# Five steps of a hybrid RWKV-7 and GLA trunk layer, moved between VectorE, ScalarE and GpSimd

## The chip, the cores and the metric

The program runs on one core of one Trainium2 chip. The metric is the device time of one execution in microseconds. Three runs of the kernel before took 932.28, 933.67 and 936.69 us; their median is 933.67.

## What is computed

One layer is computed for 128 context tokens and 512 latent tokens (640 in all, width 1024). In it the input projection is split into channels for an RWKV-7 mixer and a GLA mixer:

```python
def rwkv_mixer(r, k, v, lw, la, lg, s0, grid, p):
    rkv = short_conv(jnp.concatenate([r, k, v], axis=-1), p['rw_conv'], grid)   # 3x3 over the grid, or 3 taps
    r, k, v = jnp.split(rkv, 3, axis=-1)
    kk = heads(k * p['rw_k_k'])
    kk = kk * lax.rsqrt(jnp.sum(kk * kk, axis=-1, keepdims=True) + EPS)
    for d in range(2):
        w = jnp.exp(-RW_DECAY_SCALE * jax.nn.sigmoid(p['rw_w0'][d] + jnp.tanh(lw[d]) @ p['rw_w2'][d]))
        a = jax.nn.sigmoid(p['rw_a0'][d] + la[d] @ p['rw_a2'][d])
        ...
    bonus = (jnp.sum(rh * kh * p['rw_r_k'], axis=-1, keepdims=True) * vh).reshape(B, T, RW_W)
    return (yn + bonus) * g, ...
def gla_mixer(q, k, v, og, lgk, s0, p):
    ...
    o = rmsnorm(outs[0] + outs[1], p['gla_norm_g']).reshape(B, T, GLA_V_W)
    return o * jax.nn.silu(og), ...
```

Then follow the output projection, a residual, a second norm and a mixture of 16 experts of which each token uses two. The change touches the squares kk*kk, the products r*k*r_k of the bonus, the running sums of the decays of direction 0, and the gate of silu.

## The kernel before

All arithmetic is fp32. Channels lie on the 128 partitions and the 640 tokens along the free axis, so r, k and v have four tiles each (r0 to r3, k0 to k3, v0 to v3) of 128x640. Each engine has one program, written out by hand in the order in which it runs; nothing plans it. Engines wait for each other on semaphores: a waiting instruction holds up all that stands behind it on its engine.

TensorE works through a list of jobs (L308 to L396). Each job fills one of the eight PSUM banks in turn, and the job eight places later may start only when the bank has been emptied by VectorE or ScalarE. The weights come in slabs of 2 MB through two slots; SyncE issues a slab's DMA when the last product of the slab that held the slot is done (L669 to L690). So the projection of v can't start before its slab, issued after k3, has landed.

For each tile of r, k and v TensorE projects a latent part (512 tokens) and a context part (128 tokens), ScalarE copies both into a bordered buffer and computes the first tap (`conv_input`), and VectorE adds the other taps: eight instructions of 128x512 (L1454) and two of 128x128 (L1455, L1456). Between these convolutions VectorE does the steps in question: it empties the rows of the conditioning matrix (`ada_turned_out`, L1388), adds the bias to the low rank outputs for w and a in either direction (`low_rank`, L1565 and L1569), and runs the decay's sums per chunk (`decay_sums`, four scans at L1362). ScalarE's `sigmoid` (three activations of 128x2560) stands between a low rank and its sums.

The four bonus products (L1791 and L1792) stand behind the first segments' products `a_and_b`, just before the convolution of v2; TensorE uses them only after v3's projection. The squares of kk (L865 to L867) are made by GpSimd, each from the tile that ScalarE has scaled with k_k (`kk_scaled`, L1073 to L1075); TensorE sums them per head in the jobs kl and kc, and ScalarE and VectorE turn the sums into the normalised kk (L1785).

The GLA output gate: VectorE clamps og into yg_b (L1460), ScalarE makes the sigmoid of it in sgm (L1094 to L1097), GpSimd multiplies yg_b by sgm (L862), and VectorE multiplies the result by the normalised GLA output (L1558). GpSimd's product stands ahead of the clearing of v's borders (L864) on its queue. The GLA chunks end with `gla_states(4)` on VectorE (L1489 to L1501), for which TensorE's last products from the GLA state wait.

Of the kernel before, what the change touches and what calls it, by code (L numbers as in the profile page):

```python
# [5 lines left out]
def trunk_program(nc, x_prompt, x_sample, state_rwkv, state_gla, c, c_ctx, norm1_g, norm2_g, w_ada, b_ada,  # L6
# [7 lines left out]
    ALU = mybir.AluOpType  # L14
    ACT = mybir.ActivationFunctionType
# [14 lines left out]
    RC = RW // P  # L30
# [28 lines left out]
    with ctx:  # L59
# [20 lines left out]
        yg_b = sb("yg_b", NT * RW)  # L80
# [14 lines left out]
        vec = sb("vec", NV1 + NV2 + 2 * KT)  # L95
# [20 lines left out]
        sq = region1[:, KT * T + RC * T:KT * T + 2 * RC * T].rearrange("p (c t) -> p c t", t=T)  # L116
        aa = region3[:, :].rearrange("p (d c t) -> p d c t", d=2, t=T)
        rT = rk_r[:, 0:RC * T].rearrange("p (c t) -> p c t", t=T)
        kT = rk_r[:, RC * T:].rearrange("p (c t) -> p c t", t=T)
        kkT = kk_b[:, :].rearrange("p (c t) -> p c t", t=T)  # L120
# [4 lines left out]
        sgm = vtok_b[:, :]  # L125
# [682 lines left out]
        def _(pool):  # L808
# [49 lines left out]
            for p in range(4):  # L858
                scaled_qk(p)
            scaled_qk(4)  # L860
            pool.wait_ge(s_sig, 3)
            tell(pool.tensor_tensor(yg_b[:, :], yg_b[:, :], sgm, ALU.mult), s_sig)  # L862
            wait_filled(pool, "gkv", NT - 1, 1)
            tell(pool.memset(raw_v, 0.0), s_rawz)  # L864
            for i in range(RC):  # L865
                pool.wait_ge(s_kk, i + 1)
                tell(pool.tensor_tensor(sq[:, i], kkT[:, i], kkT[:, i], ALU.mult), s_prod)  # L867

            def b_product(h):
                p, d, g, t = step(h)  # L870
# [95 lines left out]
        def _(act):  # L966
            own, tell, out_of = steps(act, s_act)

            def A(out, in_, func=ACT.Copy, **kw):
                return act.activation(out, in_, func, **kw)  # L970
# [102 lines left out]
            def kk_scaled(i):  # L1073
                act.wait_ge(s_conv, RC + i + 1)
                tell(A(kkT[:, i], kT[:, i], scale=vec[:, vkk + i:vkk + i + 1]), s_kk)  # L1075

            def softened(v, scale):
                own(A(v, v, ACT.Exp, scale=scale))
# [274 lines left out]
        def _(dve):  # L1353
# [31 lines left out]
            def ada_turned_out(n):  # L1385

                wait_filled(dve, "adaT", n)
                out_of(TT(modv[:, 4 * n:4 * n + 4, :], bank(("adaT", n))[:, 0:8].rearrange("p (b c) -> p b c", c=2),  # L1388
                          bc(vec[:, vb_ada + 4 * n:vb_ada + 4 * n + 4], 2, 2), ALU.add), "adaT", n)
# [59 lines left out]
            def conv(n):  # L1449
                c_, dst, lat, line, out = conv_views(n)  # L1450
                dve.wait_ge(s_tap, c_ + 1)
                for m in range(1, 9):
                    i, j = m // 3, m % 3
                    own(STT(out, lat[:, i:i + GH, j:j + GW], tap(c_, i, j), out, ALU.mult, ALU.add))  # L1454
                own(STT(dst[:, 0:P], line[:, 1:P + 1], tap(c_, 1, 1), dst[:, 0:P], ALU.mult, ALU.add))  # L1455
                tell(STT(dst[:, 0:P], line[:, 2:P + 2], tap(c_, 1, 2), dst[:, 0:P], ALU.mult, ALU.add), s_conv)  # L1456
# [97 lines left out]
            dve.wait_ge(s_grs, 1)  # L1554
            own(TT(go4, go4, bc(grs20, 2, DV), ALU.mult))
            own(TT(go4, go4, bc(gng, 1, NT * GH_N), ALU.mult))
            dve.wait_ge(s_sig, 4)
            tell(TT(yg_b[:, :], yg_b[:, :], cl_b[:, RC * T:2 * RC * T], ALU.mult), s_gdone)  # L1558
            def low_rank(key, d):

                buf, off = (cl, vw0) if key == "w" else (aa, va0)
                for i in range(RC):
                    wait_filled(dve, key + "l", d, i)
                    q = off + d * RC + i
                    out_of(TS(buf[:, d, i, P:T], bank((key + "l", d, i))[:, :], vec[:, q:q + 1], -40.0, ALU.add, ALU.max), key + "l", d, i)  # L1565
                wait_filled(dve, key + "c", d)
                for i in range(RC):
                    q = off + d * RC + i
                    ins = TS(buf[:, d, i, 0:P], bank((key + "c", d))[:, i * P:(i + 1) * P], vec[:, q:q + 1], -40.0, ALU.add, ALU.max)  # L1569
                    if i < RC - 1:  # L1570
                        own(ins)
                out_of(ins, key + "c", d)
                tell(dve.memset(small[:, 2:3], 1.0), s_wx)

            def decay_sums(d):
                dve.wait_ge(s_wm, 2 * d + 1)
                for i in range(RC):
                    chunk_sums(cl[:, d, i], d)
                tell(dve.memset(small[:, 2:3], 1.0), s_cl)
# [182 lines left out]
            def start_columns(d):  # L1762
                own(dve.memset(segs[d].E1[:, :, 0:1], 1.0))
                tell(dve.memset(segs[d].E1[:, :, HD + 1:HD + 2], 1.0), s_seg)
            conv("k0")
            dve.wait_ge(s_lgt, 2)
            tell(TS(tlw, tlw, -2.0, 1.0, ALU.mult, ALU.add), s_lora)
            conv("k1")
            ada_turned_out(8)
            dve.wait_ge(s_gout, 64)  # L1770
            low_rank("w", 0)
            conv("k2")
            ada_turned_out(9)
            low_rank("a", 0)
            conv("k3")
            ada_turned_out(10)
            low_rank("w", 1)
            decay_sums(0)
            conv("v0")
            ada_turned_out(11)  # L1780
            low_rank("a", 1)
# [6 lines left out]
            a_and_b(0)  # L1788
            conv("v1")
            a_and_b(1)  # L1790
            for i in range(RC):  # L1791
                tell(STT(prod[:, i], rT[:, i], vec[:, vrk + i:vrk + i + 1], kT[:, i], ALU.mult, ALU.mult), s_bon)  # L1792
            conv("v2")
            conv("v3")
            wait_filled(dve, "bonus")
# [1012 lines left out]
```

## Time and profile before

| | us |
|---|---|
| median of three runs | 933.67 |
| the profiled execution | 932.11 |
| its span, first to last instruction | 929.60 |
| TensorE busy | 843.8 (91%) |
| VectorE busy | 565.2 (61%) |
| ScalarE busy | 331.2 (36%) |
| GpSimd busy | 156.0 (17%) |

The span is a few microseconds shorter than the time of its execution. All moments that are told are microseconds from the start of the span. The mean granted clock of TensorE over the profiled execution is 0.975 of full speed (2.4 GHz); the records know two levels, full and half (1.2 GHz). All edits lie between 200 and 390 us: the GLA part ends near 250, k's projections and convolutions follow until 312, v's until 381, and the RWKV chunk loop starts near 385.

### The profile page before, as it was taken

Reading aid. Unit: us, or ns where it says so; the run is one execution under the profiler, and the core shown is the slowest. Engines: PE = TensorE matmul, PEld = TensorE weight load, DVE = VectorE, ACT = ScalarE, POOL = GpSimd, SP = SyncE. Lnnn points to the kernel's source line nnn. Section 1 sums busy time; section 2 is a strip of 40 time slices with the busy share of each in tenths; the row PEclk is TensorE's granted clock in tenths of the full one; section 3 lists DMA queues with packets and bytes.
Section 4 is the critical chain, followed back from the end, with each engine's and each line's share of the span. In section 5 each row is a group of like instructions: output and inputs, shape, how many; then the busy total and the mean of one; then the engine's idle time right before and its main releaser. Section 6 shows DMA issues by size and latency. Waiting matters only on the chain.

```text
span 929.6 us, 21447 instructions
## 1 busy us (share of the span) xinstructions
PE 843.8 (91%) x8858; PEld 518.1 (56%) x8858; DVE 565.2 (61%) x940; ACT 331.2 (36%) x582; POOL 156.0 (17%) x302
## 2 busy tenths in 40 slices
PE   2899999999999989788888888899995999999995
PEld 0555455556555545677777777645663544444442
DVE  2533046689997889656565665697355344444467
ACT  3231111142034656556666663212310222222213
POOL 7000111113000104422222241010001000000051
PEclk9999999999999998999999999999995999999998
DMA  9923223223253201212121122691244899999856
GB/s 332 345 85 105 91 91 103 91 92 115 70 203 135 91 0 29 41 21 50 31 52 29 36 35 52 208 364 46 84 166 153 281 361 364 368 368 371 310 138 227
DMA packets 121007, 142.54 MB, mean 153 GB/s; under 512 B 50092, under 2 KB 86472, under 8 KB 120520
## 3 DMA queue, kind: packets, MB, share of 16 engines
q1 hardware_dynamic: 112072, 116.65, 38.1%
q0 software_dynamic: 3744, 13.63, 4.8%
q10 hardware_dynamic: 5088, 10.82, 3.1%
q8 instruction: 73, 1.20, 0.5%
q14 instruction: 30, 0.25, 0.1%
HBM read 123.08 MB, written 18.00 MB: 152 GB/s over the span
## 4 chain that ended last, share of the span: by engine, by line
PE 77%; DVE 12%; issue 4%; DMA 3%; ACT 3%; SPq 0%; ACTq 0%; DVEq 0%; POOLq 0%
PE bank L2040 70%; PE bank L2044 7%; DMA region<-in_w_ada_dram 3%; DVE rk_r L1454 2%; DVE region L1454 1%; ACT region L970 1%; DVE rk_r L1455 1%; DVE cl_b L1362 1%; DVE cl_b L1959 1%; DVE region L2029 1%; ACT ada_row_buffers L970 1%; DMA rk_r<-h_rows_dram,slot_tokens 0%; DVE region L2025 0%; ACT w_sb L970 0%; DVE region L2008 0%
## 5 line engine op out<-in xcount | busy, mean ns | idle before, releaser
L2040 PE MATMUL bank<-region 64*64 64x64 f32 (+3 forms) x3900 | 397.9, 297 | 15.4 <-issue 6.3
L2040 PEld LDWEIGHTS bank<-region 64*64 64x64 f32 (+1 forms) x3900 | 231.6, 148 | 168.3 <-issue 158.5
L970 ACT ACTIVATE region<-bank 128x256 f32<-128x256 f32 (+3 forms) x215 | 97.2, 452 | 341.7 <-PE bank L2040 255.1
L2040 PE MATMUL bank<-region,rk_r 128*128 128x512 f32 x176 | 79.8, 607 | 0.8 <-issue 0.8
L2044 PE MATMUL bank<-ident,region 128*128 128x128 f32 (+2 forms) x403 | 61.6, 281 | 14.0 <-DMA region<-in_c_dram 11.1
L2044 PEld LDWEIGHTS bank<-ident,region 128*128 128x128 f32 (+2 forms) x403 | 43.9, 141 | 32.0 <-issue 23.0
L2007 DVE TENSOR_SCALAR region<-region 128x256 f32<-128x256 f32 x16 | 4.7, 294 | 93.3 <-ACT region L970 93.3
L1454 DVE SCALAR_TENSOR_TENSOR rk_r<-region,vec,rk_r 128x512 f32<-128x512 f32 x64 | 50.1, 783 | 9.5 <-ACT rk_r L970 7.3
L2040 PEld LDWEIGHTS bank<-region,rk_r 128*128 128x128 f32 x176 | 33.5, 196 | 39.4 <-issue 38.2
L945 POOL DMA_INDIRECT rk_r<-h_rows_dram,slot_tokens x16 | 15.9, 992 | 227.1 <-PE bank L2044 127.2
L1636 DVE TENSOR_TENSOR region<-bank,region 128x256 f32<-128x256 f32 x60 | 25.5, 424 | 41.0 <-PE bank L2040 39.8
L2040 PE MATMUL bank<-scratch,region 64*64 64x64 f32 (+1 forms) x688 | 42.9, 230 | 4.3 <-DVE region L1645 2.9
L2040 PE MATMUL bank<-vtok_b,region 64*64 64x64 f32 x928 | 44.3, 222 | 2.5 <-DVE region L1665 1.6
L2040 PE MATMUL bank<-region,scratch 64*64 64x128 f32 (+1 forms) x512 | 35.8, 409 | 10.2 <-DMA region<-in_w_ada_dram 8.7
L2040 PEld LDWEIGHTS bank<-scratch,region 64*64 64x64 f32 (+1 forms) x688 | 40.6, 143 | 6.0 <-issue 6.0
L2040 PEld LDWEIGHTS bank<-vtok_b,region 64*64 64x64 f32 x928 | 41.3, 138 | 3.0 <-DVE region L1636 1.7
L970 ACT ACTIVATE region<-region 128x256 f32<-128x256 f32 (+1 forms) x27 | 24.7, 915 | 43.5 <-DVE region L1471 42.8
L970 ACT ACTIVATE ada_row_buffers<-bank 128x512 f32<-128x512 f32 x29 | 17.3, 597 | 53.8 <-PE bank L2044 49.6
L2040 PE MATMUL bank<-cl_b,ada_row_buffers 128*128 128x512 f32 x80 | 35.8, 596 | 0.1
L877 POOL TENSOR_TENSOR region<-kk_b,region 128x512 f32<-128x512 f32 x10 | 13.0, 1302 | 134.9 <-PE bank L2044 103.8
L2040 PE MATMUL bank<-rk_r,ada_row_buffers 128*128 128x512 f32 x80 | 35.6, 593 | 0.0
L2040 PE MATMUL bank<-cl_b,rk_r 128*128 128x512 f32 x80 | 35.2, 592 | 0.0
(283 smaller groups left out, 1130.4 us busy)
## 6 DMA issues: line engine op xcount, KB each, us to landing
region<-in_moe_w_dram SPq DMA_DIRECT2D x38, 1024.0 KB, 10.0
region<-in_w_ada_dram SPq DMA_DIRECT2D x12, 2048.0 KB, 8.6
region<-in_w_in_dram SPq DMA_DIRECT2D x6, 2048.0 KB, 8.5
cl_b<-in_moe_w_dram SPq DMA_DIRECT2D x10, 1024.0 KB, 10.8
expert_rows_dram<-yg_b ACTq DMA_DIRECT2D x14, 512.0 KB, 6.9
region<-late_condition_dram SPq DMA_DIRECT2D x3, 1024.0 KB, 9.3
a_rows_dram<-region SPq DMA_DIRECT2D x20, 128.0 KB, 2.5
region<-inverse_rows_dram SPq DMA_DIRECT2D x20, 128.0 KB, 3.1
```

What stands on the lines that cost most here:

```text
L877: tell(pool.tensor_tensor(g.b, kkT[:, :, tok], aa[:, d, :, tok], ALU.mult), s_t1)
L945: pool.indirect_dma_start(out=xg[:, i % 3], out_offset=None, in_=h2_dram, in_offset=bass.IndirectOffsetOnAxis(ap=idx[:, e:e + 1], axis=0)) ...
L970: return act.activation(out, in_, func, **kw)
L1362: own(dve.tensor_tensor_scan(u, scanm[:, :], u, 0.0, ALU.mult, ALU.add))
L1454: own(STT(out, lat[:, i:i + GH, j:j + GW], tap(c_, i, j), out, ALU.mult, ALU.add))
L1455: own(STT(dst[:, 0:P], line[:, 1:P + 1], tap(c_, 1, 1), dst[:, 0:P], ALU.mult, ALU.add))
L1636: out_of(TT(dst[:, hp::2], bank((n, h, hp))[:, 0:RC * HD].rearrange("p (h i) -> p h i", h=RC), src[:, hp::2], ALU.add), n, h, hp)
L1959: tell(STT(acc[:, t], x1[:, t], rstd[:, t:t + 1], fg, ALU.mult, ALU.mult), s_yout)
L2007: own(TS(sg[:, s], sg[:, s], 1.0, None, ALU.add))
L2029: out_of(TT(v, v, bank(("sel", r, t, h))[:, :], ALU.add), "sel", r, t, h)
L2040: return pe.matmul(out, lhsT, rhs, start=start, stop=stop)
L2044: return pe.transpose(out, in_, ident[0:n, 0:n])
```

## The change

The product of the silu gate goes from GpSimd's program to VectorE's, directly ahead of the product with the GLA output. GpSimd's four squares go; ScalarE makes each square itself, with the scaling inside the activation, behind the scaled copy that is still needed. Three of the four bonus products stand each behind a convolution of k; the fourth keeps its place. The decay sums of direction 0 stand ahead of the convolution of k3 and no longer behind the low rank that follows it.

```diff
@@ gpsimd
             scaled_qk(4)
-            pool.wait_ge(s_sig, 3)
-            tell(pool.tensor_tensor(yg_b[:, :], yg_b[:, :], sgm, ALU.mult), s_sig)
             wait_filled(pool, "gkv", NT - 1, 1)
             tell(pool.memset(raw_v, 0.0), s_rawz)
-            for i in range(RC):
-                pool.wait_ge(s_kk, i + 1)
-                tell(pool.tensor_tensor(sq[:, i], kkT[:, i], kkT[:, i], ALU.mult), s_prod)
@@ scalar
             def kk_scaled(i):
                 act.wait_ge(s_conv, RC + i + 1)
                 tell(A(kkT[:, i], kT[:, i], scale=vec[:, vkk + i:vkk + i + 1]), s_kk)
+                tell(A(sq[:, i], kT[:, i], ACT.Square, scale=vec[:, vkk + i:vkk + i + 1]), s_prod)
@@ vector
             own(TT(go4, go4, bc(gng, 1, NT * GH_N), ALU.mult))
-            dve.wait_ge(s_sig, 4)
+            dve.wait_ge(s_sig, 3)
+            own(TT(yg_b[:, :], yg_b[:, :], sgm, ALU.mult))
             tell(TT(yg_b[:, :], yg_b[:, :], cl_b[:, RC * T:2 * RC * T], ALU.mult), s_gdone)
@@ vector
+            def bonus_product(i):
+                tell(STT(prod[:, i], rT[:, i], vec[:, vrk + i:vrk + i + 1], kT[:, i], ALU.mult, ALU.mult), s_bon)
             conv("k0")
+            bonus_product(0)
             dve.wait_ge(s_lgt, 2)
             tell(TS(tlw, tlw, -2.0, 1.0, ALU.mult, ALU.add), s_lora)
             conv("k1")
+            bonus_product(1)
             ada_turned_out(8)
             dve.wait_ge(s_gout, 64)
             low_rank("w", 0)
             conv("k2")
             ada_turned_out(9)
             low_rank("a", 0)
+            bonus_product(2)
+            decay_sums(0)
             conv("k3")
             ada_turned_out(10)
             low_rank("w", 1)
-            decay_sums(0)
             conv("v0")
             ada_turned_out(11)
             low_rank("a", 1)
@@
             conv("v1")
             a_and_b(1)
-            for i in range(RC):
-                tell(STT(prod[:, i], rT[:, i], vec[:, vrk + i:vrk + i + 1], kT[:, i], ALU.mult, ALU.mult), s_bon)
+            bonus_product(RC - 1)
             conv("v2")
```

## Rows read from the trace of the kernel before

**Rows 1.** The page: the chain that ended last, share of the span.
```profile
PE 77%; DVE 12%; issue 4%; DMA 3%; ACT 3%; SPq 0%; ACTq 0%; DVEq 0%; POOLq 0%
```

**Rows 2.** Busy us by engine in a stretch; then clock, DMA share, GB/s.
```profile
275.00:300.00 25.00, 25.00 (x99) 13.04 (x98) 20.75 (x34) 11.32 (x11) 2.32 (x2) 1.00 0.48 168
```

**Rows 3.** TensorE's timeline: start, us, line, operation, [idle before, released by].
```profile
227.28 11.96 PE L2040 MATMUL bank<-region 64*64 64x128 f32 x96
239.17 0.65 PE L2040 MATMUL bank<-cl_b,region 64*64 64x128 f32 x8
241.99 1.47 PE L2040 MATMUL bank<-cl_b,region 64*64 64x128 f32 x24 [2.17 <-DVE cl_b L1501]
...
274.24 4.59 PE L2040 MATMUL bank<-lora_b,w_sb 64*128 64x512 f32 x16
...
311.41 8.92 PE L2040 MATMUL bank<-region 128*128 128x512 f32 x32 [0.56 <-DMA region<-in_w_in_dram]
...
331.73 3.71 PE L2040 MATMUL bank<-region,blk 128*128 128x512 f32 x14 [0.75 <-DVE mod L1388]
...
350.46 22.07 PE L2040 MATMUL bank<-region 64*64 64x64 f32 x128 [3.80 <-DVE region L1593]
```

**Rows 4.** GpSimd's timeline, the product and two of the squares.
```profile
215.77 5.74 POOL L862 TENSOR_TENSOR yg_b<-yg_b,vtok_b 128x2560 f32<-128x2560 f32 x1 [20.67 <-ACT vtok_b L970]
...
276.06 1.50 POOL L867 TENSOR_TENSOR region<-kk_b 128x640 f32<-128x640 f32 x1 [44.13 <-ACT kk_b L970]
...
322.89 1.66 POOL L867 TENSOR_TENSOR region<-kk_b 128x640 f32<-128x640 f32 x1 [6.46 <-ACT kk_b L970]
```

**Rows 5.** VectorE's timeline from r1's convolution to the normalised kk.
```profile
216.09 5.57 DVE L1455 SCALAR_TENSOR_TENSOR rk_r<-region,vec,rk_r 128x128 f32<-128x128 f32 x1
...
233.56 0.69 DVE L1489 TENSOR_TENSOR cl_b<-bank,cl_b 128x512 f32<-128x512 f32 x1
...
262.65 2.82 DVE L1558 TENSOR_TENSOR yg_b<-yg_b,cl_b 128x2560 f32<-128x2560 f32 x1
265.51 6.26 DVE L1454 SCALAR_TENSOR_TENSOR rk_r<-region,vec,rk_r 128x512 f32<-128x512 f32 x8
...
272.58 0.49 DVE L1767 TENSOR_SCALAR lora_b<-lora_b 128x640 f32<-128x640 f32 x1
273.33 7.13 DVE L1454 SCALAR_TENSOR_TENSOR rk_r<-region,vec,rk_r 128x512 f32<-128x512 f32 x8 [0.25 <-ACT rk_r L970]
...
289.34 6.26 DVE L1454 SCALAR_TENSOR_TENSOR rk_r<-region,vec,rk_r 128x512 f32<-128x512 f32 x8 [3.09 <-ACT rk_r L970]
...
305.35 6.27 DVE L1454 SCALAR_TENSOR_TENSOR rk_r<-region,vec,rk_r 128x512 f32<-128x512 f32 x8 [3.96 <-ACT rk_r L970]
...
317.44 6.07 DVE L1362 TENSOR_TENSOR_SCAN cl_b<-scratch,cl_b 128x640 f32<-128x640 f32 x4
...
323.66 6.94 DVE L1454 SCALAR_TENSOR_TENSOR region<-region,vec 128x512 f32<-128x512 f32 x8
...
342.87 2.82 DVE L1785 SCALAR_TENSOR_TENSOR kk_b<-kk_b,region 128x2560 f32<-128x2560 f32 x1
```

**Rows 6.** One line's instructions (L1792): duration ns min/median/max, starts, forms.
```profile
L1792 DVE SCALAR_TENSOR_TENSOR vtok_b<-rk_r,vec x4: 884/885/1774, 359.9 to 363.5; 128x640 f32<-128x640 f32 x4
```

**Rows 7.** ScalarE's timeline: a sigmoid, v0's first taps, a scaling, the exponential.
```profile
291.09 7.08 ACT L970 ACTIVATE cl_b<-cl_b 128x2560 f32<-128x2560 f32 x3
...
320.73 1.16 ACT L970 ACTIVATE region<-region,vec 128x512 f32<-128x512 f32 x2
321.92 0.83 ACT L970 ACTIVATE kk_b<-rk_r,vec 128x640 f32<-128x640 f32 x1
...
339.15 2.34 ACT L970 ACTIVATE region<-region 128x2560 f32<-128x2560 f32 x1
```

**Rows 8.** TensorE alone in a stretch: busy us, clock, DMA share, GB/s.
```profile
349.99:356.81 6.82, 6.35 (x39) 0.50 0.01 2
...
394.36:397.77 3.41, 3.00 (x65) 0.50 0.02 5
```

## The prediction

> **What bounds the kernel now.** I read the page's chain of waits first, then the busy time by stretch, then the timelines of TensorE, VectorE, GpSimd and ScalarE over 200 to 400 us, where all edits lie. Over the whole span the chain is 77% TensorE and 12% VectorE [rows 1], and in the middle of the edited stage TensorE is busy all 25 of 25 us while VectorE is busy for 20.75 [rows 2]. So a microsecond taken off VectorE is worth something only where TensorE stands still for it, and I look for TensorE's gaps. Up to the first scores of the RWKV part there are four [rows 3]: 2.17 us before 241.99, released by VectorE's last GLA state step (L1501); 0.56 us before 311.41 for the weights of v; 0.75 us before 331.73, released by VectorE's L1388, the emptying of one PSUM bank that the kl products need; 3.80 us before 350.46 for VectorE's L1593, behind ScalarE's and GpSimd's work on v1 and the decays. All other TensorE work between is back to back.
>
> The largest thing that the edits touch stands in GpSimd's rows: the product yg_b*sgm (L862) runs 215.77 to 221.51, 5.74 us [rows 4]. VectorE's L1455, a 128x128 step that elsewhere takes 0.35, takes 5.57 us over the same stretch [rows 5]. So VectorE loses 5.22 us there, and as its timeline shows no idle time from there to 241.9, all of it lies on the way to L1501, for which TensorE waits. The first square on GpSimd (L867 at 276.06, 1.50 us) does it on a small scale: the eight taps of k1 take 7.13 instead of the 6.27 of k3's, 0.87 more; the fourth (322.89) gives v0's taps 6.94, 0.67 more [rows 4, 5].
>
> The Trainium skill (SBUF — State Buffer, "Who interferes with whom") says that a VectorE instruction with two SBUF inputs and a GpSimd one that reads SBUF exclude each other, the later one waiting for the whole of the other. By that rule the first square would cost VectorE its full 1.50; the rows show 0.87, and where page and row differ the row decides. It doesn't change the sum, but it is why the product's removal counts 5.22 and not its 5.74.
>
> **The change part by part.**
>
> (a) *Product off GpSimd.* VectorE gets 5.22 back: its L1501, which released TensorE at 241.99, would do so at 236.8. TensorE's GLA chunks and lw projection end and the first state products come at 239.17, and it stands from 239.82 [rows 3]. So the wait of 2.17 goes and TensorE is then the late one, by about 3 us: worth 2.17, not 5.22. L1489, which begins that set of steps, needs a bank that TensorE fills at about 228.5 (estimate: 24 of the first 64 of the 96 products from 227.28, at some 50 ns each); VectorE comes there at 233.56 − 5.22 = 228.3, so about 0.2 of its lead is lost.
>
> (b) *The same product on VectorE,* ahead of L1558. Not shown before; the nearest row is L1558 itself, same shape and both inputs in SBUF, 2.82 us [rows 5]. Bounds: 2.8, and 5.74 if it ran as slowly as on GpSimd. I take 2.82 plus 0.04 of issue. The one short wait of VectorE before L1558 is for ScalarE's answer to VectorE's own reduction, so it shifts whole. conv k0 starts at 265.51 − 5.22 + 2.86 = 263.15.
>
> (c) *Bonus product 0, after k0.* The four took 884 ns at the least, 885 in the median and 1774 beside GpSimd's k product [rows 6]. I take 0.92 with issue; bounds 0.88 and 1.77. k0's conv takes 7.03 (265.51 to the end of L1456), so L1767 ends at 263.15 + 7.03 + 0.92 + 0.53 = 271.6. The first low rank products need it; TensorE reached them at 274.24 and now reaches them at 272.07. Slack 0.4: nothing lost. This is the tightest point. At 1.77 TensorE would lose 0.4; at 5.74 for (b) it would lose 2.5.
>
> (d) *Bonus product 1, after k1.* k1's taps, with their input 2.17 earlier, start behind L1767 at 271.7 and take 6.27, the square being gone from GpSimd. With 0.92 and the low rank's steps (4.8) VectorE is free at 284.6. conv k2 waited 3.09 for its first taps until 289.34 and now waits until 287.17. Covered by that wait: nothing.
>
> (e) *Bonus product 2 and the decay sums, before k3.* conv k2, one turned row and the low rank take VectorE from 287.17 to 299.2, bonus product 2 to 300.1. The sums wait for ScalarE's sigmoid: it took 7.08 from 291.09 [rows 7], and shifts to end near 296.0, so there is no wait. The scans take 6.07 [rows 5], to 306.3. conv k3 began at 305.35 after 3.96 of waiting; its input is now there at 303.2, and it begins at 306.4, 1.1 later than before. What hangs on it is bank adaT10, emptied at 313.7; TensorE needs it for the context half of v0, which I put at 309.24 + 7.1 = 316.4 (estimate: 512 of 640 columns of the 8.92 us at 311.41). Covered by 2.7 us. The second low rank for w ends at 318.4 instead of 317.4, and conv v0, which began at 323.66 behind the scans, begins with its input: ScalarE ended it at 321.89, now 319.7. Seven microseconds are lifted off VectorE in front of v0 and 3.9 of that shows, as v0 now waits for its input.
>
> (f) *Bank adaT11.* conv v0 runs 319.8 to 326.8 and L1388 ends at 327.0 instead of 331.59. TensorE wants the bank at 330.98 − 2.17 = 328.8. The wait of 0.75 goes. The wait for v's weights stays: that load is issued when k3's projection is done, and shifts with it.
>
> (g) *Squares on ScalarE.* Each is an activation of 128x640; the nearest rows are the scaling itself (0.83 at 321.92, x4) and the 1.25 to 1.66 of GpSimd's squares. I take 0.85, so ScalarE does 3.4 us more. The first three lie in its idle time ahead of the next projection. The fourth pushes the second w sigmoid to 321.4 to 328.5; the sums for it begin at 332.1: nothing. The kl products end at 332.5 (from 335.44, less 2.92), the logarithms and the exponential of 2.34 that ended at 341.49 end at 338.6; VectorE's second sums end at 338.2, so L1785 starts at 338.6 instead of 342.87. From there VectorE waits for ScalarE's v1, which waits for TensorE: shifted by 2.92.
>
> (h) *Three bonus products fewer before v2.* They took 3.5 of VectorE (884 + 885 + 1774), the last starting at 363.5 [rows 6]. As v2's input comes by way of TensorE, 2.92 earlier and no more, they now become waiting: nothing, unless TensorE is faster (first rival). With no gain here the bounds are 0 and 3.5 − 2.92 = 0.6.
>
> Sum: 2.17 + 0.75 = 2.92 us. The wait of 3.80 before 350.46 stays as long as it is. Every later load is issued on TensorE's or VectorE's progress, so the shift should reach the end. The profiled execution took 932.11 (span 929.60), so 929.2. The median shown is 933.67, 1.56 above it; I carry that over: 930.7.
>
> **The rivals.**
>
> *Clock gained at L0.* After the 3.80 gap TensorE ran at a granted 0.50, the 1.2 GHz level, for 6.82 us with 6.35 busy [rows 8]. The gap stays in the changed kernel. If the clock stays at 2.4 GHz, 3.2 us of that work is saved, and here (h) counts: v2's input then comes that much earlier too, and VectorE can take it, being free at 359.9 − 2.9 + 0.9 = 357.9, where the kernel before is held by its bonus products to 364.4. Time 930.7 − 3.2 = 927.5. Against it: the same gap stands in the same place. The Trainium skill (TensorE: Matmul & The Clock Gate, "What's actually happening") says that the chip's watch over activity runs free of the kernel's start; by that rule the drop comes in some runs and not in others, before and after alike. No single profile can show this. Chance 0.2.
>
> *Gain given back at the low rank.* If (b) or (c) takes its upper bound, TensorE waits for L1767 by up to 2.5, the 2.17 is gone, and what remains is 0.75 less 0.3: 933.2. For it: slack of only 0.4. Against: GpSimd, the one engine that stretches such rows, is idle there. Chance 0.1.
>
> *Slower: the clock in what follows.* The place is the chunk loop after 385 us, with many short gaps, and the products at the new places of the gaps. A half clock stretch of 3.41 us, as the one from 394.36 (3.00 busy at 0.50) [rows 8], costs up to 1.7 where TensorE is the chain. It decides from two such stretches more than before; three give 930.7 + 5.1 = 935.8, slower than before. For it: short gaps stand all through that loop. Against: the change moves no work there. Chance 0.08.
>
> The forecast keeps 0.62. What a measurement of this kernel can tell from no change is about 0.5%, 4.7 us, so 929.0 and 938.3 are the bounds. Faster takes the first rival (0.2) and a little of the forecast's own spread of 2 us (0.07): 0.27. Slower by that much needs five stretches: 0.06. The rest is 0.67. The range 926.8 to 934.8 takes in the first two rivals and not all of the third.
>
> **What would show it.** L1455 at r1 takes 0.35, and the new product 2.82 behind L1556. TensorE has no gap near 240 and none before the kl products. conv k3 starts a microsecond or so behind its input with no wait, conv v0 waits for ScalarE, and TensorE's wait before L0 stays near 3.8. L0 starts near 347.5. I am wrong if TensorE waits for L1767, or if v0's context half waits for L1388.

## The result and the profile after

The changed kernel took 927.00 us in the median of 6 runs (925.48 to 929.97), beside 933.81 (932.28 to 936.69) for 6 runs of the kernel before. The ratio is 0.9944, with a 95% interval of 0.9921 to 0.9966: about 5.2 us less (3.2 to 7.4); the two medians themselves lie 6.8 apart. The forecast was 3 us less, at 930.7; 927.0 lies in its range, 0.2 above the lower end. The profiled execution took 928.46, with a span of 925.8, beside the 932.11 and 929.60 of before. The share of the chain of waits by engine, from the page of the kernel after (that of before is [rows 1]):

```profile
PE 83%; DVE 5%; DMA 4%; ACT 3%; issue 3%; SPq 0%; ACTq 0%; DVEq 0%; POOLq 0%
```

VectorE falls from 12% of the chain to 5%. (The page of `product_only` below shows these same shares at a time within 0.2% of before's, so they don't price the change.) TensorE's timeline after (start, us, engine, line, operation, tiles, count, and in brackets the idle time before and what ended it), the rows that answer to [rows 3]:

```profile
239.98 1.91 PE L2041 MATMUL bank<-cl_b,region 64*64 64x128 f32 x32
241.81 17.57 PE L2041 MATMUL bank<-region 128*128 128x512 f32 x64
...
273.14 4.56 PE L2041 MATMUL bank<-lora_b,w_sb 64*128 64x512 f32 x16 [0.41 <-issue]
...
310.32 8.92 PE L2041 MATMUL bank<-region 128*128 128x512 f32 x32 [0.60 <-DMA region<-in_w_in_dram]
328.87 4.49 PE L2041 MATMUL bank<-region,blk 128*128 128x512 f32 x16
...
348.38 20.67 PE L2041 MATMUL bank<-region 64*64 64x64 f32 x128 [3.80 <-DVE region L1590]
```

The 8 and 24 narrow state products are one block of 32 with no gap in it. The wait ahead of the kl products is gone. The waits for v's weights and ahead of L0 are as they were. There is one new gap, 0.41 before the low rank's products. The trace puts it down to "issue", but the products need what VectorE's L1767 writes. VectorE's timeline after, beside [rows 5]:

```profile
216.90 0.35 DVE L1451 SCALAR_TENSOR_TENSOR rk_r<-region,vec,rk_r 128x128 f32<-128x128 f32 x1
...
229.74 0.69 DVE L1485 TENSOR_TENSOR cl_b<-bank,cl_b 128x512 f32<-128x512 f32 x1 [0.61 <-PE bank L2041]
...
258.83 2.83 DVE L1554 TENSOR_TENSOR yg_b<-yg_b,vtok_b 128x2560 f32<-128x2560 f32 x1
...
271.63 0.89 DVE L1763 SCALAR_TENSOR_TENSOR vtok_b<-rk_r,vec 128x640 f32<-128x640 f32 x1
272.55 0.49 DVE L1767 TENSOR_SCALAR lora_b<-lora_b 128x640 f32<-128x640 f32 x1
288.22 6.26 DVE L1450 SCALAR_TENSOR_TENSOR rk_r<-region,vec,rk_r 128x512 f32<-128x512 f32 x8 [2.17 <-ACT rk_r L965]
301.23 6.07 DVE L1358 TENSOR_TENSOR_SCAN cl_b<-scratch,cl_b 128x640 f32<-128x640 f32 x4
307.45 6.26 DVE L1450 SCALAR_TENSOR_TENSOR rk_r<-region,vec,rk_r 128x512 f32<-128x512 f32 x8
320.90 6.26 DVE L1450 SCALAR_TENSOR_TENSOR region<-region,vec 128x512 f32<-128x512 f32 x8 [1.40 <-ACT region L965]
327.98 0.17 DVE L1384 TENSOR_TENSOR mod<-bank,vec 128x8 f32<-128x8 f32 x1
```

The small step of r1 takes 0.35 instead of 5.57. The gated product takes 2.83. L1767 ends at 273.04, and TensorE's first low rank product follows at 273.14; that is the 0.41 gap. The scans stand before conv k3, which then begins with no wait, and conv v0 waits for ScalarE.

In absolute times the trace of the change is 0.8 us late already at 51 us, behind the start-up, where nothing was edited. So from here on each product of TensorE is compared with the same product (by its number) in the trace of before, less the difference at 51 us (the last column is the end of the span):

| shift against before, us | at 247 | first low rank | k3's projection | kl | L0 | loop's start, 391 | end |
|---|---|---|---|---|---|---|---|
| the change | -2.39 | -1.93 | -1.93 | -2.88 | -2.88 | -3.60 | -4.69 |
| the change, second trace | -2.39 | -1.93 | -1.93 | -2.84 | -2.83 | -2.36 | -4.08 |
| before, second trace | 0 | 0 | 0 | 0 | 0.00 | -1.03 | +0.13 |

At these places up to L0 the two traces of each kernel agree to 0.05 us, and the gain there is 2.88 and 2.83 where 2.92 was forecast. Behind L0 the traces of one kernel differ by more than a microsecond, and both traces of the change end better than they stood at L0, by 1.8 and 1.2 us.

### The profile page after: what moved, and what is told of

Its sections match the earlier page's. It is cut to its first block, busy times and chain, and to the rows that moved or that the text cites. A ratio compares the mean times of both kernels' runs of the same rounds, so it can differ in the third digit from the quotient of the medians.

```text
span 925.8 us, 21442 instructions
## 1 busy us (share of the span) xinstructions
PE 846.4 (91%) x8858; PEld 520.2 (56%) x8858; DVE 560.4 (61%) x941; ACT 334.8 (36%) x586; POOL 143.1 (15%) x297
## 4 chain that ended last, share of the span: by engine, by line
PE 83%; DVE 5%; DMA 4%; ACT 3%; issue 3%; SPq 0%; ACTq 0%; DVEq 0%; POOLq 0%
PE bank L2041 76%; PE bank L2045 7%; DMA region<-in_w_ada_dram 3%; ACT region L965 2%; DMA region<-in_w_in_dram 1%; DVE region L1450 1%; ACT ada_row_buffers L965 1%; DVE cl_b L1960 1%; DVE region L2030 1%; DMA rk_r<-h_rows_dram,slot_tokens 0%; DVE region L2026 0%; ACT w_sb L965 0%; DVE region L2009 0%; DVE region L1641 0%; DVE region L1642 0%
## 5 line engine op out<-in xcount | busy, mean ns | idle before, releaser
L2041 PE MATMUL bank<-region,scratch 64*64 64x128 f32 (+1 forms) x512 | 37.8, 426 | 8.3 <-DMA region<-in_w_ada_dram 6.7
```

What stands on the lines that cost most here:

```text
L2041: return pe.matmul(out, lhsT, rhs, start=start, stop=stop)
```

## The experiments

In the first two groups of runs each kernel was timed in 5 rounds beside the kernel before. The ratios come from these, the shifts from one trace each, taken as in the table. The median of before was 934.70 (929.33 to 940.00, 35 runs) for the first four kernels below and 933.64 (928.32 to 938.17, 24 runs) for the second four. The last four have one run each, beside one of before at 933.19; a single time can't tell them apart, so only their traces are read.

### The product alone (`product_only`)

The kernel before with only step (a) and (b):

```diff
-            pool.wait_ge(s_sig, 3)
-            tell(pool.tensor_tensor(yg_b[:, :], yg_b[:, :], sgm, ALU.mult), s_sig)
...
-            dve.wait_ge(s_sig, 4)
+            dve.wait_ge(s_sig, 3)
+            own(TT(yg_b[:, :], yg_b[:, :], sgm, ALU.mult))
```

> The kernel before with one edit: the silu product on VectorE ahead of L1558, not on GpSimd. My theory: this edit alone gives the 2.2 to 2.4 us at 242; the squares on GpSimd still stretch v0's taps, so a wait for L1388 before the kl products stays near 0.6, and VectorE's bonus products still stand before v2. TensorE reaches the first L scores 2.2 to 2.5 earlier than in the kernel before, start-up differences taken out. Rival (the clock did it all): the start of k0's projection does not move by more than 0.5 against the end of the r3 projection.

Measured: 932.62, ratio 0.9985 (0.9966 to 1.0005). In the trace the shift is the full -2.39 up to the w low rank and k3's projection. Then it falls to -1.46 at kl and L0, where 2.2 to 2.5 earlier was expected. TensorE's timeline of this kernel at v's projection, and TensorE alone by stretch (start and end, length, busy, granted clock, DMA share, GB/s):

```profile
311.81 10.55 PE L2039 MATMUL bank<-region 128*128 128x512 f32 x32 [0.84 <-DMA region<-in_w_in_dram]
```

```profile
311.73:315.14 3.41, 3.33 (x4) 0.50 0.02 5
```

The same 32 products took 8.92 after a gap of 0.56 in before [rows 3] and 10.55 here: the clock was granted at 0.50, the 1.2 GHz level, in the first 3.41 us. So the GLA gap was worth what was forecast, and 1.6 us of it went to the clock at a place where nothing had been edited. As TensorE comes that much later, the wait of some 0.6 that was expected ahead of kl isn't there, which gives 0.9 back. Whether that fall comes in every execution of this kernel isn't known from one trace.

### The bonus products back before v2 (`bonus_back`)

The change with products 0 to 2 taken out of their new places:

```diff
-            bonus_product(0)
...
-            bonus_product(1)
...
-            bonus_product(2)
...
-            bonus_product(RC - 1)
+            for i in range(RC):
+                bonus_product(i)
```

> The changed kernel with its first three bonus products back in front of v2. My theory: the 0.41 before the first low rank products goes, and what the changed kernel had at the L scores stays (2.9, or 0.4 better). The products then hold v2's taps: from the start of the L0 scores the taps of v2 begin 14.0 us later at the earliest, whatever the clock, where the changed kernel began them at 12.9 with 3.4 us of half clock. So it loses 1.1 of it with a half clock stretch of 3.4, nothing with one of 6.8, and 2.5 to 3 with none. Rival (VectorE's work before v2 is hidden, only the clock differs): v2's taps wait for ScalarE as in the changed kernel.

Measured: 931.38, ratio 0.9969 (0.9947 to 0.9991). The 0.41 gap is gone, and L0 is at -3.32. VectorE's timeline of this kernel:

```profile
356.72 4.54 DVE L1763 SCALAR_TENSOR_TENSOR vtok_b<-rk_r,vec 128x640 f32<-128x640 f32 x4
361.30 6.26 DVE L1450 SCALAR_TENSOR_TENSOR region<-region,vec 128x512 f32<-128x512 f32 x8
369.53 6.26 DVE L1450 SCALAR_TENSOR_TENSOR region<-region,vec 128x512 f32<-128x512 f32 x8 [1.19 <-ACT region L965]
```

and of the change:

```profile
361.24 6.26 DVE L1450 SCALAR_TENSOR_TENSOR region<-region,vec 128x512 f32<-128x512 f32 x8 [2.55 <-ACT region L965]
370.72 6.26 DVE L1450 SCALAR_TENSOR_TENSOR region<-region,vec 128x512 f32<-128x512 f32 x8 [2.44 <-ACT region L965]
```

Counted from the start of L0 (347.28 here, 348.38 in the change), v2's taps start 14.02 in this kernel and 12.86 in the change, 1.16 later. v3's taps start 22.25 and 22.34. So the products do hold v2, at the 14.0 that I expected. But what v2 loses is taken back from the wait before v3: behind v's last tap (379.6 in before) the shift is -3.44, beside -3.38 and -2.88 in the change's two traces, so the loss of 1.1 didn't come. That agrees with step (h) for the stretch up to there. In the timings this kernel is nonetheless 0.25% above the change, with intervals that overlap. Its trace loses 4.2 us in the loop, from -4.3 at 391 to -0.1 at 587, and has two half-clock stretches of 3.41 us there (418.92 and 439.40) that the change's traces don't have.

### Bonus product 0 behind L1767 (`bonus0_later`)

```diff
-            bonus_product(0)
             ...
             tell(TS(tlw[:, :], ...), s_lora)
+            bonus_product(0)
```

> The changed kernel with bonus product 0 behind the low rank's input (L1767) instead of ahead of it. My theory: L1767 is then 0.92 earlier, TensorE's 0.41 gap before the first low rank products of w goes, and everything to the L scores shifts by 0.4; the total 0.4 better, which the timing can't show but the moment of each product can. Rival: the 0.41 is TensorE's own issue and stays.

Measured: 929.79, ratio 0.9949 (0.9927 to 0.9971). TensorE's timeline (the second row ends with its window, not with its products):

```profile
270.12 1.92 PE L2041 MATMUL bank<-region,scratch 128*32 128x512 f32 x16
271.97 4.25 PE L2041 MATMUL bank<-lora_b,w_sb 64*128 64x512 f32 x13
```

The gap is gone, and the shift of -2.39 is kept through the low rank where the change has -1.93. So product 0 did hold up TensorE. The timings can't show 0.45.

### L0's clock, with three unused products in the 3.80 gap (`l0_filled`)

```diff
             project("v1", w, P)
+            b = open_early("L", 0, 0)
+            for n in range(3):
+                mm(b[:, :], blk[:, :], hT[:, n, P:T])
```

> The changed kernel with three products of 128x512 that nothing uses in TensorE's 3.8 us gap before the L0 scores (into the bank that L0 then overwrites). My theory: the clock stays at 2.4 GHz there, so v2's and v3's projections come 1.4 to 3.2 earlier than with a half clock stretch, and VectorE, free of three bonus products, can take them: 1.5 to 3 better at the turning of v, and the runs with no stretch there no better. Rival (VectorE or ScalarE bound there): the clock is full but v3's last tap ends as before, counted from L0.

Measured: 930.52, ratio 0.9953 (0.9930 to 0.9976). TensorE's timeline of this kernel (a row that ends with its window), and its stretch from L0 on (columns as above):

```profile
347.73 2.61 PE L2041 MATMUL bank<-region 64*64 64x64 f32 x36 [1.22 <-DVE region L1590]
```

```profile
347.73:368.41 20.68, 20.68 (x146) 1.00 0.19 33
```

beside TensorE's first stretch at L0 in the change:

```profile
348.93:352.34 3.41, 3.41 (x16) 0.50 0.03 5
```

The clock stays at 1.00, the 2.4 GHz level, all through. v3's taps start 20.68 after L0 instead of 22.34, and the last of v is at -5.94 instead of -3.38 (its turning, 379.6 in before). But by the loop's end (587) the shift is only -0.38. The expected gain came, 2.6 us at v, and was then lost in the loop.

### The change once more (`after_again`)

> The changed kernel unaltered, for its own spread. The first six timings gave 0.9944 (0.9921 to 0.9966) to the kernel before; bonus0_later, which differs by one product's place, gave 0.9949. My theory: the change is worth the 2.5 to 2.9 us counted on TensorE at the L scores, some 0.997, and what lies beyond is the spread of the half clock stretches; the ratio comes out between 0.995 and 0.998. Rival: a real further gain behind the L scores; the ratio stays at 0.9945 or below.

Measured: 928.50 (926.27 to 931.05, 7 runs), ratio 0.9943 (0.9923 to 0.9963). My theory's 0.995 to 0.998 doesn't hold; the first six timings were no accident. In the timings some 2.3 us come on top of the 2.9 counted at L0.

### The product back on GpSimd (`product_back`)

The change with the four lines of the first experiment reversed.

> The changed kernel with the silu product back on GpSimd. My theory: VectorE's L1451 in r1 takes 5.6 us again, TensorE waits 2.1 to 2.2 at 242, and of the 2.4 gained there nothing is left; the wait for L1384 before the kl products stays away, so the L scores come 0.7 to 1.0 earlier than in the kernel before (start-up taken out). No wait at the first low rank products, since VectorE has one 2.8 us product less ahead of them and TensorE comes later. Rival (the gain is VectorE's lighter load in k and v): L scores stay 2.5 or more earlier.

Measured: 933.73, ratio 1.0001 (0.9975 to 1.0027). VectorE's and TensorE's timelines of this kernel, and the stretch behind the gap:

```profile
217.12 5.56 DVE L1453 SCALAR_TENSOR_TENSOR rk_r<-region,vec,rk_r 128x128 f32<-128x128 f32 x1
```

```profile
243.02 2.16 PE L2042 MATMUL bank<-cl_b,region 64*64 64x128 f32 x24 [2.18 <-DVE cl_b L1499]
245.11 20.05 PE L2042 MATMUL bank<-region 128*128 128x512 f32 x64
```

```profile
243.30:250.13 6.83, 6.83 (x30) 0.50 0.00 0
```

The stretched 0.35 step and the gap are back with the product, so it is their cause. The price is more than the gap: in both traces of before the clock stays full behind that gap, and here it falls, so that the shift is +3.18 where it is 0 in before, and +2.42 at L0, where 0.7 to 1.0 earlier was expected. With the rest of the change in place, the product's place is worth 0.58% (1.0001 against 0.9943), about 5.4 us, all that the change gains.

The parts don't add up to the whole, though: by the timings the product alone is worth 0.15%, the rest alone nothing, and both together 0.56%, each give or take 0.2 to 0.3. On TensorE's timeline the gaps do add. What doesn't is the clock, which in the trace of either part falls at a place where the change keeps it, and takes back 1.6 us (`product_only`) or 3 (here).

### Three tiny products in the same gap (`l0_tiny`)

As `l0_filled`, with 2 columns in place of 512. These are the same instructions in the same place, but they fill nothing.

```diff
+                mm(b[:, 0:2], blk[:, :], hT[:, n, P:P + 2])
```

> The changed kernel with three products of 2 columns in place of the three of 512 in the gap before L0: as many instructions on TensorE, next to no work. In l0_filled the turning of v came 3.4 us earlier than in the changed kernel (counted from the same start), and from 385 to 585 us it lost 5 again, in waits put down to issue that stood every 123 or 124 products. Theory A (the added instructions move the places at which TensorE's program is fetched, to where no other wait hides it): the loop from 385 to 585 takes 4 to 5 us more than in the changed kernel here too, with the same spacing. Theory B (an earlier or faster start of the loop is absorbed): here the loop takes as long as in the changed kernel, within 1 us and its half clock stretches.

Measured: 931.73, ratio 0.9987 (0.9967 to 1.0007): 0.44% above the change by the ratios and 3.2 us by the medians of the same group, for three products that take 0.73 us of a gap. The gap stays at 3.24, L0 is at -2.64 and at half clock (6.83 us from 346.87), and the loop's start is at -2.86. Then the loop from 391 to 587 takes 199.7 us, where it takes 196.8 and 194.7 in the two traces of the change. From TensorE's timeline of the loop:

```profile
418.92 0.34 PE L2041 MATMUL bank<-region,ada_row_buffers 64*64 64x64 f32 x7 [1.08 <-issue]
...
424.21 0.46 PE L2041 MATMUL bank<-region 64*64 64x64 f32 x15 [0.30 <-issue]
```

and of the change, in the same part (the last row is from its second trace):

```profile
411.01 0.28 PE L2041 MATMUL bank<-scratch,region 64*64 64x64 f32 x2 [0.40 <-issue]
...
419.68 0.21 PE L2041 MATMUL bank<-region,ada_row_buffers 64*64 64x64 f32 x1 [0.46 <-issue]
...
418.53 0.21 PE L2041 MATMUL bank<-region,ada_row_buffers 64*64 64x64 f32 x1 [1.01 <-issue]
```

Counted from 0 at the program's start (the three added products are six records), waits for "issue" stand at the numbers 2708, 2954, 3696 and 5058 in before, in the change and here alike, and these numbers lie multiples of 123 or 124 apart. So they stay at their number, and added instructions give them to other products. The profile of the change has, from 400 to 560 us, these packets (count, MB) on the larger of its instruction queues:

```profile
q8 instruction: 36, 0.59, 1.5%
```

That is one in 4.4 us, in which TensorE does 123 products, which fits with a fetching of the program. How long such a wait is varies by itself: number 2954 is the row at 419.68 with 0.46 in the change, 1.01 in its second trace and in `bonus_back`, and 1.08 here. The idle time that TensorE's waits put down to issue between 385 and 590 us is 10.3 us in 21 waits in the change, 11.5 in 25 with the tiny products and 14.3 in 30 with the wide ones; but it is also 11.7 in 24 in `bonus_back`, which adds no instruction to TensorE. Over 385 to 585 us, all engines (busy and count of TensorE, its weight loads, VectorE, ScalarE, GpSimd; clock, DMA share, GB/s), in the change:

```profile
385.00:585.00 200.00, 173.19 (x5533) 151.66 (x5526) 118.92 (x220) 119.75 (x235) 55.70 (x145) 0.98 0.18 36
```

with the tiny products:

```profile
385.00:585.00 200.00, 172.01 (x5454) 150.44 (x5445) 117.01 (x216) 119.29 (x234) 55.69 (x145) 0.98 0.18 36
```

79 products fewer are done in the same 200 us. That this kernel is slower than the change is shown by the timing. Why isn't. My theory A wanted 4 to 5 us more in the loop; it is 2.9 and 5.0 more than in the change's traces, but `bonus_back`, with as many instructions as the change, takes 200.7 there. The fetching of TensorE's program, whose points fall on other products, is a reading that the rows allow; the spread of one trace is its rival, and neither was tried by itself.

### The latent gate's products behind v1 (`lg_behind_v1`)

This kernel fills the gap before L0 with work that is needed anyway. It also has the edit of `bonus0_later`.

```diff
-            gate_inputs(range(5, KT)).then_inc(s_lgl, 1)
             project("v1", w, P)
+            gate_inputs(range(5, KT)).then_inc(s_lgl, 1)
...
-            act.wait_ge(s_lgl, 1)
-            out_of(A(slg[:, P:T], bank(("pl", "lg"))[:, :]), "pl", "lg")
             ... (growths_for_b(0))
+            act.wait_ge(s_lgl, 1)
+            out_of(A(slg[:, P:T], bank(("pl", "lg"))[:, :]), "pl", "lg")
```

> The changed kernel with bonus product 0 behind L1767 and with the last three products of the latent gate input (k 5 to 7) behind v1's projection, not ahead of it; ScalarE empties their bank behind the first growths. TensorE issues as many instructions as in the changed kernel. My theory: v1 comes 2.9 earlier and the three products fill the gap before L0, which shrinks from 3.8 to about 1; L0 comes 2.5 to 2.9 earlier than in bonus0_later, the clock stays full there, the turning of v comes 3.5 to 5 earlier than in the changed kernel, and the loop keeps its length: ratio to the kernel before 0.991 to 0.994. Rival (something else holds L0: VectorE's kk or the first segment's product on GpSimd): L0 moves by less than 1.

Measured: 924.41 (921.87 to 927.70, 6 runs), ratio 0.9898 (0.9873 to 0.9924). It beats both kernels, the change by 0.45%, and is better than the 0.991 to 0.994 expected. TensorE's timeline and stretch of this kernel:

```profile
308.79 10.61 PE L2041 MATMUL bank<-region 128*128 128x512 f32 x32 [0.61 <-DMA region<-in_w_in_dram]
...
349.30 19.18 PE L2041 MATMUL bank<-region 64*64 64x64 f32 x128 [1.24 <-DVE region L1590]
```

```profile
349.30:370.00 20.70, 20.61 (x144) 1.00 0.19 33
```

The gap is 1.24 instead of 3.80 and L0 runs at the full clock, in 19.18 instead of 20.67. I expected L0 earlier than in `bonus0_later`; in this trace it is 2.2 later (-0.88 against -3.04). TensorE fell to half clock at 308.93 for 3.41 us, after the short wait for v's weights, and at 322.58 for 6.83; these 10.24 us cost at most 5.1 (an estimate), more than enough to hide the 2.5 to 2.9 expected. From L0 to the end it gains 5.2 more.

### The decay sums back, then sums and squares (`sums_back`, `sums_squares_back`)

First the sums alone, then the squares too, taken out of the change:

```diff
-            decay_sums(0)
...
             (low_rank("w", 1))
+            decay_sums(0)
```

```diff
+            for i in range(RC):
+                pool.wait_ge(s_kk, i + 1)
+                tell(pool.tensor_tensor(sq[:, i], kkT[:, i], kkT[:, i], ALU.mult), s_prod)
...
-                tell(A(sq[:, i], kT[:, i], ACT.Square, scale=vec[:, vkk + i:vkk + i + 1]), s_prod)
```

> The changed kernel with the decay sums of direction 0 back behind the second low rank of w. Counted from its input, k3's convolution in the kernel before ended in L1388 after 26.24 us, and TensorE wanted the bank after 25.63; the square on GpSimd put 0.67 into the first number. My theory: without the square it is 25.57, so sums back alone brings no wait at the kl products (0.1 at most), and k3's taps start with their input again; L scores as in the changed kernel. Rival (the sums' new place is what took the wait away): 0.6 to 0.8 of waiting returns ahead of the second kl product.

> The changed kernel with the decay sums back behind the low rank and the four squares back on GpSimd. My theory: GpSimd's fourth square stretches v0's taps by 0.6 to 0.7 again and the wait for L1388's bank before the kl products is there again, 0.5 to 0.8 long; the L scores come 0.7 to 1.0 later than in sums_back (start-up and clock taken out). Rival (VectorE has slack of more than a microsecond there): no wait.

Measured: 928.28 and 930.59, beside 933.19. With the sums back the shift is -2.61 from kl to L0, 0.27 short of the change's -2.88. With the squares back as well it is -1.93. TensorE's and VectorE's timelines of the second:

```profile
329.76 3.71 PE L2043 MATMUL bank<-region,blk 128*128 128x512 f32 x14 [0.71 <-DVE mod L1386]
```

```profile
321.69 6.94 DVE L1452 SCALAR_TENSOR_TENSOR region<-region,vec 128x512 f32<-128x512 f32 x8
```

The wait for bank adaT11 is back in its old size only when both are back, and v0's taps take 6.94 again where they take 6.26 with the squares on ScalarE. Of the 0.95 at kl the sums, taken back first, bring 0.27 (a wait of 0.11 and a slower start behind it) and the squares, taken back on top, 0.68. I had expected at most 0.1 for the sums. The squares alone weren't taken back. In the change L1384 has emptied the bank at 328.14 and TensorE comes to it at 329.73, so I estimate that a stretch of 0.68 alone would bring no wait: either of the two steps removes most of the wait, and the order in which they are undone decides which seems to do it.

### Before and `product_back` once more (`before_again`, `product_back_2`)

> The kernel before once more, for where its clock falls. The gap of 2.17 at 242 was followed by the full clock in its first profile; in product_back the same gap of 2.18 was followed by 6.83 us at half clock, which cost another 3.4. My theory: the fall after that gap comes in some executions and not in others, so with this profile and product_back_2 it is seen at least once more or at least once missing, and no gap's length tells which. Rival (it belongs to product_back): it is missing here and present in product_back_2.

> product_back unaltered, a second profile. My theory: a gap of 2.1 to 2.2 at 242 again; the half clock stretch behind it may or may not be there. Rival (it belongs to product_back): it is there again, 6.83 us long.

Measured: 932.68 and 933.19. TensorE's timeline of before, second trace, then that of `product_back`, second trace, with the stretch behind:

```profile
242.12 1.47 PE L2040 MATMUL bank<-cl_b,region 64*64 64x128 f32 x24 [2.17 <-DVE cl_b L1501]
```

```profile
242.34 2.40 PE L2042 MATMUL bank<-cl_b,region 64*64 64x128 f32 x24 [2.17 <-DVE cl_b L1499]
```

```profile
241.91:248.74 6.83, 6.37 (x29) 0.50 0.00 0
```

The same gap of 2.17 is followed by full clock in two traces of two of before and by 6.83 us at half clock in two of two of `product_back`; there it costs 2.9 and 3.2 us. Four traces don't tell whether the fall belongs to the kernel or comes by chance in some executions of either. That stays open.

## Why the prediction was right, step by step

*(a) and (b), the product.* Right in mechanism and nearly in size. L1451 takes 0.35, the new product 2.83 where 2.82 was taken, and the gap before the state products is gone. The shift is -2.39, 0.22 more than the gap's length; that comes with the state products now running as one block. With the product back on GpSimd, stretch and gap come back. The small step waited for nearly all of GpSimd's instruction each time. The Trainium skill (SBUF — State Buffer, "Who interferes with whom") calls the ports that the two engines share an exclusive lock. The trace agrees, and with the squares too, where the prediction saw a difference: it took the rule to cost VectorE the square's full 1.50. A tap that starts behind the square waits only for what is left of it. VectorE's timeline of before, the tap that meets the first square and the one that meets the fourth [rows 4]:

```profile
276.48 1.62 DVE L1454 SCALAR_TENSOR_TENSOR rk_r<-region,vec,rk_r 128x512 f32<-128x512 f32 x1
...
323.66 1.43 DVE L1454 SCALAR_TENSOR_TENSOR region<-region,vec 128x512 f32<-128x512 f32 x1
```

The squares end at 277.56 and 324.55, the taps 0.55 later each time; the 0.35 step ends 0.15 behind the product. So each ends behind GpSimd's instruction by 0.20 less than its own length (0.75 for a tap).

*(c), the tightest point.* Wrong by 0.45: TensorE waits 0.41 for L1767, and `bonus0_later` takes the wait away. The failed term is the lead lost at L1489, now L1485. It waits 0.61 for its bank where 0.2 was worked out from the product count, and not even the 0.2 went into the 263.15 at which step (b) let conv k0 start. TensorE came 0.22 earlier than forecast besides, so the slack of 0.4 became a wait of 0.4. This is a small part of the second rival: neither the product nor the bonus product took its upper bound.

*(d), (e).* Right. conv k2 waits 2.17 for its taps, conv k3 starts at 307.45 behind the scans with no wait, conv v0 waits 1.40 for ScalarE, and v0's context half isn't held.

*(f), (g).* Right in mechanism. The wait at kl is gone, worth 0.95 and 0.91 in the two traces, not 0.75, again somewhat more than the gap's length. I named the sums and v0's earlier start as its cause and left out the squares; the runs show that with the sums back, the squares' place still removes most of the wait. The squares cost ScalarE 0.83 each, and no wait on TensorE came from them. ScalarE's timeline after, the fourth square and the second w sigmoid, which step (g) put at 321.4 to 328.5:

```profile
321.70 0.83 ACT L965 ACTIVATE region<-rk_r,vec 128x640 f32<-128x640 f32 x1
322.56 7.08 ACT L965 ACTIVATE cl_b<-cl_b 128x2560 f32<-128x2560 f32 x3
```

*(h).* Right up to the turning of v: nothing, by `bonus_back`; what its timing lacks lies in the loop. In the first rival it was wrong. With L0 at full clock in `l0_filled`, v2's taps started 12.69 after L0, 1.6 earlier than the 14.26 of before and not 3.2. ScalarE was what v2 waited for, and the gain of 3 showed only at v3 (20.68 instead of 23.73).

*The sum.* 2.92 forecast; -2.88 and -2.83 at L0, as the two gaps were worth 0.22 and 0.19 more than their length, which covers the 0.45 lost in (c). Not forecast is the rest, some 2.3 of the 5.2 us that the timings give. The lower end of the range was set by a rival that didn't happen (927.5 with the clock gained at L0), so that 927.0 still lies in the range is in part luck; the mechanism up to L0 isn't. Putting the product back takes all of the 5.2 away. A part may be the clock behind the 2.17 gap. The 59 runs of before that stood beside the first eight experiments have a median of 934.3, some 2 us above its two profiled executions (932.11 and 932.68), and neither of those shows the fall that both of `product_back` show, at 3 us each. If some of before's runs have that fall, removing the gap gains more than the gap. The mean granted clock of each run fits with that: worked out from it, the 59 runs of before spend 51.1 us at half clock in the mean and the 13 of the change 47.3. Half clock costs at most half its time, so these 3.8 us are worth at most 1.9 (an estimate). Where they lie in the runs without a trace isn't known, so that they lie behind the 2.17 gap is argued, not shown; no trace of before has the fall in it. Another part may be the loop and the router behind it, where the change's traces end 1.8 and 1.2 better than at L0, while one of before's two traces moved by 1 us there without any edit.

*The rivals.* "Clock gained at L0" didn't happen: both traces of the change have half clock at L0, 3.41 us from 0.55 behind its start in the first and 6.83 from 1.6 ahead of it in the second, and so has each of the eleven traces with the gap of 3.80. `l0_filled` and `lg_behind_v1`, with 1.22 and 1.24, don't. "Given back at the low rank" came at 0.45. The slower one, more half-clock stretches in the loop, is seen in the trace of `bonus_back` (13.65 us of them between 391 and 587, where before has 3.41) but not in the change (6.83 and 0), where the shift at the loop's end (587) is -3.25 and -4.09.

## What to carry to other kernels

A long two-input instruction on GpSimd can be priced by the VectorE instruction that it stretches: look for a small one whose duration matches the large one's, follow it to the engine that bounds, and count only that engine's gap. Then look at the granted clock behind each gap, because the gap's price can double there. When instructions are added to a full TensorE program, time the same instructions with almost no work in them too: a kernel with three such products lost most of this change's gain. And before a wait is put down to an edit, look for it in a second trace of the unaltered kernel.

## What the runs showed of the hardware

- A 5.74 us product on GpSimd held a 0.35 us VectorE step for 5.57 us; a 1.66 us square of the same engine, which had begun 0.77 before the tap, held VectorE for 0.68. The step ended 0.15 behind GpSimd's instruction, the taps of 0.75 us 0.55 behind it.
- A TensorE gap of 2.17 us was followed by full clock in two traces and by 6.83 us at 1.2 GHz in two others. Waits for a DMA of only 0.84 and 0.61 before v's projection were followed by 3.41 us at that level, while those of the other twelve traces, 0.53 to 0.90, were not; the length alone doesn't decide it.
- Gaps of 3.80 before L0 came with such a stretch in all eleven traces that have them, and so did one of 3.24 behind three products of 2 columns; gaps of 1.22 and 1.24 did not.
- In the loop TensorE waited for "issue" at numbers of products that lie multiples of 123 or 124 apart and are the same in all kernels compared (2708, 2954, 3696, 5058), for 0.2 to 1.9 us. The wait at 2954 took 0.46 us in one trace of the change and 1.01 in the other. A kernel with three products of 2 columns added ahead of the loop was 0.44% slower; why isn't shown.
